# Seven block products in place of eight for 18 gate/up pairs of the last feed-forward network of a two-layer hybrid encoder

## The reference, cut to what matters

```python
D_MODEL, SEQ, D_FF = 1024, 512, 2816

def swiglu(h, w_gu, w_down):
    g, u = jnp.split(h @ w_gu, 2, axis=-1)
    return (jax.nn.silu(g) * u) @ w_down

h = modulate(rms_norm(x), sh3, sc3)
x = x + 0.5 * g3[:, None, :] * swiglu(h, ffn2_w_gu[i], ffn2_w_down[i])
x = rms_norm(x, post_gain[i])
```

## Time and profile before

| | us |
|---|---|
| median of 3 runs | 1982.16 |
| the runs | 1980.74 to 1982.25 |
| span of the profiled execution | 1979.4 |

### The profile page before, as it was taken

How to read it: one execution, slowest core, us unless ns; L and a number is a source line. 1 busy time by engine, 2 the same in 40 slices (tenths; PEclk the granted TensorE clock), 3 DMA queues, 4 the chain that set the end, 5 groups by cost and what they waited for, 6 DMA issues and landing times.

```text
span 1979.4 us, 23447 instructions
## 1 busy us (share of the span) xinstructions
PE 1951.1 (99%) x9060; PEld 1620.7 (82%) x9060; DVE 1142.1 (58%) x1720; ACT 720.1 (36%) x1068; POOL 212.1 (11%) x245
## 2 busy tenths in 40 slices
PE   6999999999999999999999999999999999999998
PEld 5888888888888888888888888878888888888887
DVE  7665564799857655645864453586554573333335
ACT  5222222464743213224422221356565452223134
POOL 3110000017701100100110000001101000000000
PEclk9999999999999999999999999999999999999999
DMA  8665552322126655622564443233322233222322
GB/s 336 227 215 172 197 191 96 106 89 86 33 64 223 204 185 183 235 81 89 172 200 138 165 155 116 91 101 113 96 86 86 62 103 106 103 88 94 97 80 69
DMA packets 76350, 263.97 MB, mean 133 GB/s; under 512 B 8897, under 2 KB 11073, under 8 KB 76274
## 3 DMA queue, kind: packets, MB, share of 16 engines
q1 hardware_dynamic: 55296, 190.34, 29.0%
q0 software_dynamic: 20256, 72.02, 11.1%
q10 hardware_dynamic: 722, 0.61, 0.1%
HBM read 260.66 MB, written 2.13 MB: 133 GB/s over the span
## 4 chain that ended last, share of the span: by engine, by line
PE 94%; DVE 3%; POOL 1%; issue 1%; DMA 0%; ACT 0%; SPq 0%; DVEq 0%; ACTq 0%; POOLq 0%
PE bank L1495 30%; PE bank L1500 29%; PE bank L1496 29%; PE bank L1943 1%; DVE dve_tmp L1068 1%; PE bank L1960 1%; PE bank L1875 1%; PE bank L1719 1%; DVE h_lo L1059 1%; PE bank L1721 1%; PE bank L1720 1%; PE bank L1932 0%; PE bank L1850 0%; DVE wlo L871 0%; POOL rstd L389 0%
## 5 line engine op out<-in xcount | busy, mean ns | idle before, releaser
L1495 PE MATMUL bank<-h_hi,whi 128*128 128x512 f32 x1808 | 711.3, 393 | 5.4 <-ACT h_hi L553 2.8
L1496 PE MATMUL bank<-h_hi,wlo 128*128 128x512 f32 x1808 | 705.1, 390 | 0.0
L1500 PE MATMUL bank<-h_lo,whi 128*128 128x512 f32 x1808 | 593.6, 390 | 2.4 <-POOL h_lo L405 2.4
L507 ACT ACTIVATE whi<-wraw 128x1024 fp32r<-128x1024 f32 x338 | 347.0, 1053 | 267.4 <-PE bank L1500 263.9
L871 DVE TENSOR_TENSOR wlo<-wraw,whi 128x1024 fp32r<-128x1024 f32 x324 | 388.9, 1223 | 60.1 <-ACT whi L507 59.8
L1495 PEld LDWEIGHTS bank<-h_hi,whi 128*128 128x128 f32 x1808 | 340.5, 188 | 78.9 <-issue 7.3
L1500 PEld LDWEIGHTS bank<-h_lo,whi 128*128 128x128 f32 x1808 | 339.7, 188 | 75.1 <-POOL h_lo L405 2.9
L1496 PEld LDWEIGHTS bank<-h_hi,wlo 128*128 128x128 f32 x1808 | 340.6, 188 | 68.7
L1495 PE MATMUL bank<-hid_hi,whi 128*128 128x512 f32 (+1 forms) x856 | 328.7, 384 | 0.0
L1500 PE MATMUL bank<-hid_lo,whi 128*128 128x512 f32 (+1 forms) x856 | 328.0, 383 | 0.0
L1496 PE MATMUL bank<-hid_hi,wlo 128*128 128x512 f32 (+1 forms) x856 | 327.9, 383 | 0.0
(11 more groups left out here) (256 smaller groups left out, 1359.5 us busy)
## 6 DMA issues: line engine op xcount, KB each, us to landing
wraw<-in_w_units_dram SPq DMA_DIRECT2D x306, 512.0 KB, 3.5
arena<-in_mod_t_dram POOLq DMA_DIRECT2D x96, 512.0 KB, 5.0
mod_tile<-in_mod_t_dram POOLq DMA_DIRECT2D x32, 512.0 KB, 4.9
wraw<-in_w_units_dram SPq DMA_DIRECT2D x32, 384.0 KB, 3.5
arena<-in_mod_t_dram SPq DMA_DIRECT2D x12, 512.0 KB, 9.6
arena<-in_w_units_dram SPq DMA_DIRECT2D x10, 512.0 KB, 4.5
xT<-in_xt_dram SPq DMA_DIRECT2D x8, 256.0 KB, 4.3
sq<-k_roots POOLq DMA_DIRECT2D x8, 256.0 KB, 3.6
```

The lines of the kernel that those rows point to most:

```text
L507: act.activation(whi[:, s % RING, :, :], wraw[:, s % RING, :, :], ACT.Copy).then_inc(hi_ready, 1)
L1495: pe.matmul(dst, whi[:, w, k, :], hi_, start=first, stop=False)
L1496: pe.matmul(dst, wlo[:, w, k, :], hi_, start=False, stop=False)
L1500: return pe.matmul(dst, whi[:, s % RING, k, :], lo_, start=False, stop=last)
```

## The change

In the last feed-forward network (`SUM_FFN`), 18 of the 22 gate/up pairs (`SUM_PAIRS`: all but the first four of the first third) are no longer made by `pair` but by `sum_pair`. Such a pair is a product of 2x2 blocks: gate and up by the two halves of the 8 rows, times the two halves of the rows by the two halves of the tokens. It is made by a scheme with 7 block products (`PRODUCTS`) in place of 8, each of 4 blocks of rows and 256 columns, with sums of blocks ahead of it on both sides:

- on the moving side, once: ScalarE writes the whole h to `full` in `arena` (`whole_h`), VectorE makes four differences (`diff_t`), which are rounded (`round_t`) and split (`split_t`);
- on the weight side, for each pair: four sums, `wcomb`. The first, low rows plus high rows of the up weights (`wcomb[:, 1]`), is made by two transfers that GpSimd issues: a copy of 256 KB from memory, and behind its semaphore one of 256 KB that adds to what is there (`accum_op=ALU.add`). The other three are VectorE's (`combine`). Raw weights and sums are split in four groups (`GROUP_OF`), for two, two, two and one product; `group_hi` rounds on ScalarE and `group_lo` subtracts on VectorE;
- on the results: ScalarE copies four of the products or partial sums out of PSUM (`one_keep`, `two_keep`, `five_keep`, `three_keep`) and the last one to `ups`; VectorE adds two of them for the up side and two 256-wide pieces for the gate side, before Silu and the product. TensorE's third product waits for `one_kept`, the fifth for `two_kept`, the sixth for `five_kept`, the seventh for `three_kept`.

`job(s)` counts a summed pair as 7 in `unit_done`, `hi_ready` and `lo_ready`. The loops of this network are written out. Cut to its core:

```diff
@@ gpsimd
             job(17, 4)
+            for n, s in enumerate(SUM_PAIRS):
+                if n:
+                    pool.wait_ge(lo_ready, place(SUM_PAIRS[n - 1]) + GROUP_OF[1][1])
+                else:
+                    pool.wait_ge(lo_ready, place(s - 4) + 1)
+                rows = w_units[s + 1, :, :].rearrange("p (k n) -> p k n", k=KT)
+                pool.dma_start(wcomb[:, 1, :, :], rows[:, low_k, :]).then_inc(low_copied, 16)
+                pool.wait_ge(low_copied, 16 * (n + 1))
+                pool.dma_start(wcomb[:, 1, :, :], rows[:, high_k, :], accum_op=ALU.add).then_inc(low_summed, 16)
@@ scalar
+            def whole_h(st):
+                v, sh, _ = modulation(st)
+                for k in range(KT):
+                    act.wait_ge(h_ready, KT * v + k + 1)
+                    act.activation(full[:, k, :], full[:, k, :], ACT.Identity, bias=modc[:, sh + k:sh + k + 1], scale=1.0)\
+                        .then_inc(h_whole, 1)
+            def sum_pair(s, tile):
+                n, j, q = SUM_PAIRS.index(s), job(s), tile % 2
+                x, _, w = sum_banks(s)
+                act.wait_ge(unit_done, j + 1)
+                act.activation(one_keep, x, ACT.Copy).then_inc(one_kept, 1)
+                next_hi(s, 0)
+                act.wait_ge(unit_done, j + 3)
+                act.activation(two_keep, x, ACT.Copy).then_inc(two_kept, 1)
+                act.wait_ge(unit_done, j + 4)
+                act.activation(five_keep, w, ACT.Copy).then_inc(five_kept, 1)
+                next_hi(s, 1)
+                act.wait_ge(unit_done, j + 5)
+                act.activation(three_keep, x, ACT.Copy).then_inc(three_kept, 1)
+                next_hi(s, 2)
+                act.wait_ge(gates_added, n + 1)
+                act.activation(act_tmp[:, q, :], act_tmp[:, q, :], ACT.Silu).then_inc(act_out, 1)
+                act.wait_ge(unit_done, j + 7)
+                act.activation(ups[:, first], x, ACT.Copy).then_inc(up_kept, 1)
+                next_hi(s, 3)
+                act.wait_ge(evicted, s + 2)
+                act.activation(hid_hi[:, tile, :], dve_tmp[:, q, :], ACT.Copy).then_inc(hid_rounded, 1)
@@ vector
+            def combine(s):
+                n, g, u = SUM_PAIRS.index(s), s % RING, (s + 1) % RING
+                a11, a12, a21 = wraw[:, g, low_k, :], wraw[:, g, high_k, :], wraw[:, u, low_k, :]
...
+                dve.tensor_tensor(wcomb[:, 2, :, :], a11, a21, ALU.subtract).then_inc(w_combined, 1)
+                dve.wait_ge(low_summed, 16 * (n + 1))
+                dve.tensor_tensor(wcomb[:, 0, :, :], wcomb[:, 1, :, :], a11, ALU.subtract).then_inc(w_combined, 1)
+                dve.wait_ge(w_combined, 4 * n + 2)
+                dve.tensor_tensor(wcomb[:, 3, :, :], a12, wcomb[:, 0, :, :], ALU.subtract).then_inc(w_combined, 2)
+            def sum_pair(s, tile, outs, rounded):
...
+                if s + 2 in SUM_PAIRS:
+                    combine(s + 2)
+                next_lo(s, 0)
+                next_lo(s, 1)
+                dve.wait_ge(five_kept, n + 1)
+                dve.wait_ge(three_kept, n + 1)
+                dve.tensor_tensor(ups[:, second], three_keep, five_keep, ALU.add).then_inc(up_added, 1)
...
@@ tensor
+            def sum_pair(s):
+                n, j = SUM_PAIRS.index(s), job(s)
+                x, z, w = sum_banks(s)
+                pe.wait_ge(evicted, s - 2)
+                for p, dst in enumerate((x, z, x, w, x, w, x)):
+                    if p == 2:
+                        pe.wait_ge(one_kept, n + 1)
...
+                    pe.wait_ge(lo_ready, j + GROUP_OF[p // 2][1])
+                    w_hi, w_lo = split_group(whi, s, p // 2), split_group(wlo, s, p // 2)
+                    for k in range(4):
+                        at = 4 * (p % 2) + k
+                        m_hi, m_lo = (m[:, k, :] for m in MOVING[p])
+                        pe.matmul(dst, w_hi[:, at, :], m_hi, start=p in (0, 1, 3) and k == 0, stop=False, skip_group_check=True)
+                        pe.matmul(dst, w_lo[:, at, :], m_hi, start=False, stop=False, skip_group_check=True)
+                        ins = pe.matmul(dst, w_hi[:, at, :], m_lo, start=False, stop=k == 3, skip_group_check=True)
+                    ins.then_inc(unit_done, 1)
```

More of the change, by code:

```diff
@@ L93, in down_tiles, with job, summed, third_start @@
     return range(first, first + 1)
+SUM_FFN = (3,)
+PLAIN_PAIRS = 4
+SUM_PAIRS = [third_units(f, t)[0] + 2 * n for f in SUM_FFN for t in range(3)
+             for n in range(0 if t else PLAIN_PAIRS, THIRDS[t][1])]
+PRODUCTS = 7
+GROUP_OF = ((0, 2), (2, 4), (4, 6), (6, 7))
+def job(s):
+    return s + (PRODUCTS - 2) * sum(a < s for a in SUM_PAIRS)
+place = job
+def summed(s):
+    return s in SUM_PAIRS or s - 1 in SUM_PAIRS
+def third_start(s):
+    return max(third_units(f, t)[0] for f in range(4) for t in range(3) if third_units(f, t)[0] <= s)
+def split_free(s):
+    if not summed(s - RING):
+        return job(s - RING) + 1
+    last = max(a for a in SUM_PAIRS if a < s)
+    return job(last) + GROUP_OF[s - last - 2][1]
+def group_free(s, g):
+    if s - 2 in SUM_PAIRS:
+        return job(s - 2) + GROUP_OF[g][1]
+    return job(s - RING + g) + 1
+def raw_free(s):
+    a = s - RING
+    if not summed(a):
+        return job(a) + 1
+    return job(a) + 6 if a in SUM_PAIRS else job(a - 1) + PRODUCTS
 def dot_at(m):
@@ L585, in up_body @@
                                                ACT.Copy).then_inc(hid_rounded, 1)
+                    if f in SUM_FFN:
+                        if t == 0:
+                            whole_h(FFN_ST[f])
+                            up_body(up, 0, 0, True)
+                            for m in range(3):
+                                round_t(m)
+                            up_body(up + 4, 0, 2)
+                            round_t(3)
+                        for tile in range(0 if t else PLAIN_PAIRS, k):
+                            sum_pair(up + 2 * tile, tile)
+                        if t < 2:
+                            for q in range(4):
+                                hi(down + q + 4)
+                            for g in range(4):
+                                group_hi(down + KT, g)
+                        else:
+                            down_stats(down, st)
+                        continue
                     if t == 0:
@@ L1149, in ffn @@
                                           ALU.subtract).then_inc(hid_ready, 1)
+                        if f in SUM_FFN and t == 0 and n == 1:
+                            for m in range(4):
+                                diff_t(m)
+                            for m in range(3):
+                                split_t(m)
+                        if f in SUM_FFN and t == 0 and n == 3:
+                            split_t(3)
                         if t == 2:
@@ L1169, in ffn @@
                             add_x(down + d, d, 0, gate)
-                            lo(down + d + 4)
+                            if d < 4 or f not in SUM_FFN:
+                                lo(down + d + 4)
+                            else:
+                                if d == 4:
+                                    combine(down + KT)
+                                group_lo(down + KT, d - 4)
                             for m in down_tiles(f, t, d):
```

177 lines of the change are left out of this document (153 added, 24 removed).

## The result

The changed kernel takes 2015.4 us (median of 4 runs, 2014.2 to 2016.3) against 1981.7 us before: the ratio is 1.0172, with a 95% interval of 1.0157 to 1.0186. It is slower by 33.8 us where 13.3 were forecast. The time lies inside the stated range of 1971 to 2022, but the change is two and a half times as large as the one forecast. The profiled execution has a span of 2012.2 us, 32.8 us over the 1979.4 before.

A forecast was written before the change was run, and what follows sets the result against it. The prediction took TensorE to bound the kernel before the change; -14.4 (TensorE), +1.6 (start) and +26.1 (loop through the transfers) gave +13.3 us, so 1995.5 us, with a range of 1971 to 2022.

The forecast's parts named there:

- TensorE's gain: Summed pairs: 84 matmuls of 256 columns replace 48 of 512, 10.08 us per pair, 0.80 less; 18 pairs give -14.4 us.
- VectorE and ScalarE hidden in throughput: Per summed pair, VectorE needs 8.0 us and ScalarE 5.8 us of TensorE's 10.08, so neither is full.
- The start: First summed pair of the first third: starts 0.2 us late, its third product 1.4 us late, together +1.6 us.
- The loop through the two transfers: Single buffer for the first weight sum: copy, adding transfer and VectorE's work set the pace; 13 rounds cost +26.1 us.
- The size of a round: One round of the two-transfer loop: 3.6 + A + 4.23, forecast as 12.1 us against TensorE's 10.08 per pair.
- the second leg: From GpSimd's issue of the adding transfer to VectorE's second sum; forecast as A = 4.3 plus 0.2 us to VectorE.
- A: The accumulating transfer of 256 KB in the loop, taken as 4.3 us, the middle of 3.7 and 4.9.
- the forecast's case: Copy and addition together take 7.2 to about 10 us; slower by 4 to 41 us, chance 0.5.
- The rule of the Trainium skill: For GpSimd's two transfers: 2.6 us for 256 KB, 3.2 for 512 KB; by it both transfers would take 5.8 us.
- rival 1: GpSimd's two transfers take 5.8 us together, a round 10.0, TensorE sets the pace: -12.8, 1969.4 us; chance 0.12.
- Rival 4: The adding transfer takes 7.2 us, for example; a round 15.0, in all +51, 2033 us; chance 0.1.
- The clock: TensorE's granted clock stays at the upper level despite idling 2 us of 12; otherwise time passes the range's upper end.

## Why the prediction was right and wrong, step by step

- **What bounds the kernel: right.** TensorE did, and does again as soon as the loop is shorter than a pair.
- **TensorE's gain, -14.4 us: right to within 1 us.** Without the loop, pairs are 10.11 us apart, not 10.08; that is 0.6 us over 18 pairs. With +1.6 us for the start the forecast for that case was -12.8 us; two buffers gave -12.6 (1970.0 against 1982.6).
- **VectorE and ScalarE hidden in throughput: right**, even with a fourth sum on VectorE.
- **The start, +1.6 us: right in all**, 0.58 + 1.01 by the wait rows, though forecast as 0.2 + 1.4, so the two errors cancel by luck. Counted by starts, as above, the two waits cost about 1.9 us.
- **The loop through the two transfers: right as a mechanism**, in its place, its 13 rounds and the two products where it shows. Without the copy, with a second buffer, and without transfers it is gone; with another order on ScalarE it is not.
- **The size of a round: wrong, and by one term.** From VectorE's split to GpSimd's issue 0.3 us, forecast 0.1; the copy with its handoff 3.5, forecast 3.8; VectorE's part 3.76, forecast 3.73; the second leg 6.1 us where A = 4.3 and a handoff of 0.2 made 4.5. That is the step that failed: "I take the middle of 3.7 and 4.9, A = 4.3"; the adding transfer took 6.2 us to land. The round became 13.6 instead of 12.1 us, and 13 x 1.5 = 19.5 us is the whole miss of the span (13.3 + 19.5 = 32.8). The legs are those of the second third; in the first third the second leg was shorter and the copy and its issue longer, and that the rounds came out alike there is not explained by A alone. The prediction saw both reasons, more bytes read and SP's fetches behind the copy, and took a value between the shortest and the median of plain fetches of 512 KB; even the median, 4.9, would have been too short. The runs give, for the second leg, 3.4 us for a plain transfer beside fetches of 64 KB, 0.8 for the addition, 1.3 for the fetches and 0.6 for both at once. Copy and addition together landed in 9.4 us, inside the 7.2 to about 10 of the forecast's case.
- **The rule of the Trainium skill** (DMA: Bandwidth & Descriptors, "Anatomy of one DMA — SWDGE (gpsimd) path"), 2.0 us plus bytes at 436 GB/s, gives as an estimate 2.6 us for 256 KB. The trace does not agree: the copies landed after 2.9 to 3.3 us, and the plain second transfers beside fetches of 64 KB after 3.4 (median), so even these two took 6.6 us together, and rival 1 with its 5.8 was out. The measurement decides.
- **Rival 4**, an accumulation slow in itself, 7.2 us: it is not. With SP's fetches small its leg was 4.2.
- **The clock: forecast wrong, without effect.** It was to stay at the upper level, or else the time would go past 2022. It fell at places (last section), and the time stayed at 2015.4.

## What to carry to other kernels

Count the rounds of a chain that goes through a single buffer, filled by transfers and freed by the engine that waits for them, and compare one round with the step of the engine that sets the pace. Here the sum of latencies decided, not the load of any engine or of the DMA, and a second buffer turned 34 us of loss into 12 us of gain. Price a transfer in such a loop with the other queue's fetches that the same loop releases at that moment, not with the median of quieter stages. A row that names the engine waited for names a place in its order; here reordering moved the wait and left the time as it was.

## What the runs showed of the hardware beyond what was expected

- An adding transfer of 256 KB occupies GpSimd for 0.87 us per issue, a plain one for 0.55, and its leg is 0.8 us longer than a plain one's when SP fetches only 64 KB a unit beside it (4.2 against 3.4).
- SP's fetches slow GpSimd's transfers (4.7 against 3.4 us, 6.1 against 4.2) and the other way round. Between 1765 and 1840 us in the changed kernel SP's 512 KB had a median of 5.0 us to landing, against 3.5 before:

```profile
wraw<-in_w_units_dram SPq DMA_DIRECT2D x10, 512.0 KB, 5.0
```

Not all of that is GpSimd's doing. From 1755 to 1805 us, first in the kernel without GpSimd's transfers, then in that with two buffers, which has all of them:

```profile
wraw<-in_w_units_dram SPq DMA_DIRECT2D x10, 512.0 KB, 3.9
wraw<-in_w_units_dram SPq DMA_DIRECT2D x10, 512.0 KB, 4.8
```

- TensorE's granted clock fell at places in the changed kernel, where TensorE waits in each round; with two buffers it was 1.00 in the same stretches. From 1640 to 1700 us it had a mean of 0.91, in the second third 1.00, and in two stretches of the last, of 14 and 8 us, 0.88 and 0.80. There matmuls of 256 columns start 0.21 us apart in place of 0.12. Columns as in rows 5:

```profile
1640.00:1700.00 60.00, 52.77 (x350) 49.69 (x350) 43.32 (x53) 30.62 (x48) 5.67 (x8) 0.91 0.40 111
1914.00:1928.00 14.00, 12.39 (x89) 12.19 (x90) 8.89 (x13) 7.00 (x12) 1.41 (x2) 0.88 0.45 115
1942.00:1950.00 8.00, 8.00 (x57) 8.00 (x57) 5.54 (x8) 3.95 (x8) 1.42 (x2) 0.80 0.52 135
```

The rounds there were no longer than elsewhere (1915.85 to 1929.28 is 13.4 us, to 1943.18 another 13.9). Where the clock falls is not the same in each execution: when the changed kernel was run again it stayed at 1.00 from 1640 to 1700 us, and fell in the second third and the last.

```profile
1640.00:1700.00 60.00, 49.35 (x351) 45.63 (x350) 43.69 (x53) 30.30 (x48) 5.67 (x8) 1.00 0.41 113
```

TensorE is busy for 3.4 us less there, waits that much longer, and has done as many matmuls (351 against 350) in the same 60 us. So in this stretch the lower clock cost nothing: TensorE had time to spare in the loop. What the clock would cost where TensorE sets the pace was not tried.
